# The first product of the gated network with both operand parts in one 512-column matmul, its halves joined by ScalarE and VectorE

## The reference, cut to what matters

```python
h = rmsnorm_2(x, norm2_g[l])
x = x + (jax.nn.silu(h @ ffn_w1[l]) * (h @ ffn_w3[l])) @ ffn_w2[l]
return rmsnorm_2(x, norm_f_g)
```

## Time and profile before

| what | value |
|---|---|
| median of three runs | 1012.93 us (1010.57 to 1013.58) |
| the profiled execution | 1013.9 us, its span 1012.1 us |
| TensorE busy | 977.0 us, 97% of the span, mean granted clock 0.985 |
| VectorE busy | 788.2 us, 78% |
| ScalarE busy | 560.6 us, 55% |
| the `ffn` stage | about 820 to 940 us of the span |

### The profile page before, as it was taken

How to read it: one execution, slowest core, us unless ns; L and a number is a source line. 1 busy time by engine, 2 the same in 40 slices (tenths; PEclk the granted TensorE clock), 3 DMA queues, 4 the chain that set the end, 5 groups by cost and what they waited for, 6 DMA issues and landing times.

```text
span 1012.1 us, 19319 instructions
## 1 busy us (share of the span) xinstructions
PE 977.0 (97%) x7468; PEld 910.6 (90%) x7468; DVE 788.2 (78%) x1370; ACT 560.6 (55%) x922; POOL 105.1 (10%) x134
## 2 busy tenths in 40 slices
PE   4799999999999999999999999999999999999996
PEld 2479998888989899999888999998889999999996
DVE  4757986999777677667876899999998887777554
ACT  3248675444655567776544666677126564444352
POOL 0000000000000000000000000999910000000000
PEclk8799999999999999999999999999999999999998
DMA  9998798887564865554555455453446555555531
GB/s 378 421 419 336 275 378 300 318 325 280 144 203 115 307 239 177 189 186 167 208 179 213 164 193 170 164 208 127 165 139 221 182 187 189 194 179 190 193 116 42
DMA packets 35880, 222.27 MB, mean 220 GB/s; under 512 B 3883, under 2 KB 9180, under 8 KB 9436
## 3 DMA queue, kind: packets, MB, share of 16 engines
q1 hardware_dynamic: 35804, 221.22, 60.6%
HBM read 220.13 MB, written 1.07 MB: 219 GB/s over the span
## 4 chain that ended last, share of the span: by engine, by line
PE 81%; DVE 8%; DMA 4%; ACT 4%; issue 2%; DVEq 0%; SPq 0%; ACTq 0%
PE bank L656 22%; PE bank L645 17%; PE bank L646 16%; PE bank L650 12%; PE bank L982 5%; PE bank L1035 3%; DMA mod_raw<-w_mod 2%; DVE w_lo L1472 2%; PE s_banks L679 1%; ACT w_hi L1109 1%; DVE s_banks L1879 1%; DVE bank L1854 1%; PE s_banks L1035 1%; DMA raw<-weights 1%; DVE ab L1847 1%
## 5 line engine op out<-in xcount | busy, mean ns | idle before, releaser
L1472 DVE TENSOR_TENSOR w_lo<-raw,w_hi 128x1024 fp32r<-128x1024 f32 x284 | 346.3, 1225 | 32.1 <-ACT w_hi L1109 29.7
L1109 ACT ACTIVATE w_hi<-raw 128x1024 fp32r<-128x1024 f32 x284 | 296.1, 1050 | 93.6 <-PE bank L656 89.9
L645 PE MATMUL bank<-xg_hi,w_hi 128*128 128x258 f32 (+1 forms) x1376 | 340.9, 285 | 0.8 <-ACT w_hi L1109 0.5
L646 PE MATMUL bank<-xg_lo,w_hi 128*128 128x258 f32 (+1 forms) x1376 | 336.5, 281 | 0.0
L645 PEld LDWEIGHTS bank<-xg_hi,w_hi 128*128 128x128 f32 x1376 | 259.7, 189 | 5.8 <-issue 4.7
L646 PEld LDWEIGHTS bank<-xg_lo,w_hi 128*128 128x128 f32 x1376 | 260.1, 189 | 0.2
L656 PE MATMUL bank<-xg_hi,w_lo 128*128 128x258 f32 (+1 forms) x1376 | 198.3, 282 | 0.3 <-DVE w_lo L1472 0.3
L656 PEld LDWEIGHTS bank<-xg_hi,w_lo 128*128 128x128 f32 x1376 | 178.5, 189 | 0.8 <-DVE w_lo L1472 0.5
L650 PE MATMUL bank<-hid,w_hi 128*128 128x512 f32 x512 | 127.7, 391 | 0.0
L650 PEld LDWEIGHTS bank<-hid,w_hi 128*128 128x128 f32 x512 | 91.5, 188 | 15.8
L656 PEld LDWEIGHTS bank<-hid,w_lo 128*128 128x128 f32 x512 | 68.5, 188 | 5.3
(11 more groups left out here) (245 smaller groups left out, 1262.0 us busy)
## 6 DMA issues: line engine op xcount, KB each, us to landing
raw<-weights SPq DMA_DIRECT2D x157, 1024.0 KB, 4.9
mod_raw<-w_mod SPq DMA_DIRECT2D x28, 1024.0 KB, 11.4
mod_raw<-w_dots SPq DMA_DIRECT2D x20, 1024.0 KB, 9.6
toep<-bias_by_distance SPq DMA_DIRECT2D x8, 256.0 KB, 5.4
x<-x_in SPq DMA_DIRECT2D x1, 1024.0 KB, 4.9
toep<-bias_by_distance SPq DMA_DIRECT2D x8, 128.0 KB, 3.9
y_out<-yout SPq DMA_DIRECT2D x4, 256.0 KB, 2.4
c_all<-c_row SPq DMA_DIRECT2D x1, 512.0 KB, 14.8
```

The lines of the kernel that those rows point to most:

```text
L645: pe.matmul(dst, hi, r_hi, start=start, stop=False, skip_group_check=True)
L646: pe.matmul(dst, hi, r_lo, start=False, stop=False, skip_group_check=True)
L1109: act.activation(pool_w_hi[:, at, :] if name == "pool" and at < 2 else w_hi[:, at % HL, :], raw[:, slot, (at % 2) * UT * P:(at % 2 + 1) * ...
L1472: ve.tensor_tensor(lo, raw[:, slot, (at % 2) * UT * P:(at % 2 + 1) * UT * P], hi.bitcast(F32), ALU.subtract).then_inc(lo_done, 1)
```

## The change

The high and low part of xg become one tile `xg[P, 2, DC, ROW]`, the high part first. In the `ffn` stage the 16 matmuls over `w_hi` become 8 of 512 columns (`by_high_once`), so that the bank holds two halves. ScalarE copies the second half into `acc2`; VectorE adds the first half to it and then scales the sum by `rstd`. The space behind xg is 64 bytes larger than before, so that `vec` and what follows start 64 bytes later.

```diff
-        half_line("xg_lo")
-        xg_lo = sb("xg_lo", [P, DC, ROW], F32R)
-        with ExitStack() as part:
-            half_line("xg_hi", part)
-            xg_hi = sb("xg_hi", [P, DC, ROW], F32R, part)
-        sb("behind_xg_hi", [P, DC * ROW + 2 * HALF])
+        half_line("xg")
+        xg = sb("xg", [P, 2, DC, ROW], F32R)
+        xg_hi, xg_lo = xg[:, 0], xg[:, 1]
+        sb("behind_xg", [P, 3 * HALF])
...
+        half_copied, halves_added = sem("half_copied"), sem("halves_added")
...
-                            by_high(dst[:, 0:n], slot, k, r_hi[:, k, 0:n], r_lo[:, k, 0:n], k == 0)
+                            if name == "ffn":
+                                by_high_once(dst[:, :], slot, k, xg[:, :, k, 0:n], k == 0)
+                            else:
+                                by_high(dst[:, 0:n], slot, k, r_hi[:, k, 0:n], r_lo[:, k, 0:n], k == 0)
...
-                    by_high(dst[:, 0:n], (U0[name] + j) % HL, k, r_hi[:, k, 0:n], r_lo[:, k, 0:n], k == 0)
+                    if name == "ffn":
+                        by_high_once(dst[:, :], (U0[name] + j) % HL, k, xg[:, :, k, 0:n], k == 0)
+                    else:
+                        by_high(dst[:, 0:n], (U0[name] + j) % HL, k, r_hi[:, k, 0:n], r_lo[:, k, 0:n], k == 0)
...
             def ffn(i, j):
+                act.wait_ge(pe_units, 8 * i + (U0["ffn"] + j + 1))
+                act.wait_ge(tile_read, 8 * i + (T0["ffn"] + j))
+                act.activation(acc2[:], out_bank("ffn", j)[:, SEQ:2 * SEQ], ACT.Copy).then_inc(half_copied, 1)
                 if j % 2 == 0:
...
                 ve.wait_ge(pe_units, 8 * i + (U0["ffn"] + j + 1))
-                ve.tensor_tensor(ab[:, j % 2, 0:SEQ], out_bank("ffn", j)[:, 0:SEQ], rstd[:, 0:SEQ], ALU.mult).then_inc(tile_read, 1)
+                bank, f = out_bank("ffn", j), ab[:, j % 2, 0:SEQ]
+                ve.wait_ge(half_copied, 8 * i + j + 1)
+                ve.tensor_tensor(acc2[:], bank[:, 0:SEQ], acc2[:], ALU.add).then_inc(halves_added, 1)
+                ve.wait_ge(halves_added, 8 * i + j + 1)
+                ve.tensor_tensor(f, acc2[:], rstd[:, 0:SEQ], ALU.mult).then_inc(tile_read, 1)
```

## The result

The changed kernel takes 1023.6 us (median of four runs, 1022.26 to 1025.91) against 1013.15 us beside it: the ratio is 1.0112, 95% interval 1.0096 to 1.0128. It is 1.1% slower, outside the stated range of 1009.5 to 1020. The profiled execution has a span of 1020.8 us, 8.7 more than before.

The account below looks back on a forecast made before the run. TensorE (97% busy) bounds the kernel; in ffn the change makes VectorE the bound. TensorE ends 2.3 us late, moved buffers count 0: 1013.9 becomes 1016.2 profiled, 1015.2 us on the median's scale, range 1009.5 to 1020.

Parts of the forecast that it names:

- The ring: In ffn, copy, addition, silu and splits between ScalarE and VectorE hold a pair of units to at least 5.88 us.
- TensorE's own unit: In ffn, 24 matmuls fall to 2.77 us with 512 columns, saving 2.2 us if TensorE stays the bound.
- Where the lateness goes: From ffn into the last product, banks and splits absorb some lateness; TensorE ends 2.3 us late.
- the split that TensorE needs last: Last ffn unit's split, making low weights for the last product's third unit; done at 949.6, TensorE 2.3 us late.
- The clock: Rival: short TensorE waits in ffn drop the clock to 1.2 GHz, up to 122 us more, 1137; chance 0.02.
- The longer ring: Rival: in ffn the scaling starts 0.56 behind the addition, 0.2 us more a pair, 1019.4 us; chance 0.24.
- TensorE as the bound: Rival: in ffn the odd copy is not held, TensorE sets the pace, 1010.7 us; chance 0.14.
- The places: Rival: moved operands run at 0.91 per eight matmuls in the last product and other stages, about 1009 us; chance 0.10.

Follow-up runs that it names:

- e3: Changed kernel, with ScalarE's silu behind its split instead of ahead of it on even units; 1011.87 us, ratio 0.9992.
- e9: Changed kernel's 512-column matmuls with the eviction of before, reading only the bank's first half (leaves out one product); 1014.4 us, ratio 1.0011.
- e2: Changed kernel, with the last product's first four output tiles in banks 4 to 7, which ffn does not use; 1016.53 us, ratio 1.0029.
- e4: Changed kernel, with 20 idle matmuls into an unused bank ahead of each of the two waits for the last banks; 1022.27 us, ratio 1.0087.
- e6: Changed kernel, with the space behind xg 64 bytes smaller, so everything behind it lies where it lay before; 1024.42 us, ratio 1.0109.
- e10: Changed kernel, with the copied half going to two scratch tiles in turns; 1024.75 us, ratio 1.011.
- e1: Kernel before, with only the buffers placed where the change puts them; 1014.48 us, ratio 1.0014.
- e7: Kernel before, with only the last product's operand (f_hi, f_lo) moved by 128 bytes, to its changed-kernel place; 1011.82 us, ratio 0.9996.
- e5: Changed kernel with the 256-column matmuls of before; ScalarE copies the sum, VectorE takes the greater of sum and copy; 1024.15 us, ratio 1.0105.
- e8: Changed kernel, silu behind the split, everything behind xg in its old place, last product's operand moved 128 bytes; 1011.38 us, ratio 0.999.
- e11: Kernel before, last product's operand moved 128 bytes and TensorE held by a wait in that product's first unit; 1013.78 us, ratio 1.0012.
- e12: Kernel before, with TensorE held by a wait in the last product's first unit, operand in its old place; 1013.49 us, ratio 1.0001.

## Why the prediction was wrong

**The ring: right.** 5.84 us a pair against 5.88, the scaling at 0.46, VectorE's wait of 0.57 against 0.67, ended by ScalarE's copy. The last unit's addition was forecast at 947.6 and stands at 948.55, of which 0.8 is the mixing product's delay ahead of it. TensorE's own unit was forecast at 2.77; free of waits it is 2.787 and `ffn` 1.45 us shorter than before (e3, e9), 0.033 a unit instead of 0.05. TensorE's waits for the low split began some twenty units into the stage (at 871.75), where I had said ten.

**Where the lateness goes: the step that failed.** The prediction said that the split of the last `ffn` unit is "the split that TensorE needs last", and put 2.3 us there. The waits for low splits came, of about that size: 2.7 us against before, all inside `ffn`. But they are not the last wait. The last product's first unit sums four output tiles at once, in the four banks that the last four `ffn` units used, so its third and fourth tile wait for the scaling of the second-last and last unit. TensorE may run four units ahead of the eviction inside `ffn`, and there it loses only 2.7 us against before; at the boundary it must have all four banks within one unit, so everything that it had run ahead is lost at once. That costs 5.4 us, for which the forecast had no term. The kernel before had the same wait, too short to notice: VectorE's last scaling ends at 940.29, and the fourth tile's first matmul runs from 940.37, with 0.20 to the next start instead of 0.12 (the unit took 2.91 for 2.83).

```profile
939.87 0.42 DVE L2050 TENSOR_TENSOR ab<-bank,rstd 128x256 f32<-128x256 f32 x1 [1.26 <-PE bank L656]
```

```profile
940.37 0.36 PE L645 MATMUL bank<-f_hi,w_hi 128*128 128x256 f32 x1
940.57 0.28 PE L646 MATMUL bank<-f_lo,w_hi 128*128 128x256 f32 x1
```

e2 takes this wait out and lands at 1016.5, near the forecast, with 2.76 us more than before in `ffn` and no wait behind it: what I forecast was about a kernel without this bank dependence.

**The clock: a chance of 0.02, and it came, in one place.** I looked at the many short waits inside the stage, where the clock did stay at 1.00. It fell in the one stretch of 5 us with two long waits, for some 7 us, of which TensorE worked the last 4 without a break, and cost 1.7 us (e4). In e6 and e10 it rose later and slowed the second unit as well (3.77 and 3.12 us). The price of 122 us that I gave it was for another event.

**The rivals.** The longer ring would have given 1019.4 by a price (0.56) that the trace refutes (0.46). TensorE as the bound is what e3 shows once the order is changed. The places came within the bounds, both ways: 0.8 and twice 0.5 us lost, 2.2 us won back in the profiled execution, though e1 and e7 show that the place alone does not win them. The mixing product, whose 0.91 for eight was the good case of that rival, itself went to 0.94.

**What it sums to.** On the scale of the profiled executions the forecast was +2.3. Measured are 2.7 in `ffn`, 5.4 the wait at the boundary, 1.7 the clock, 0.8 the mixing product, 1.0 the two `down`, less 2.2 in the last product: 9.6 before rounding. The span shows 8.7, since the other stages took 0.9 less in this execution. The timed runs show more, a ratio of 1.0112 or 11 us. The same sum over the stages is 9.5 us in e5, 10.9 in e6 and 12.1 in e10, the other profiled kernels with this ring: it varies with the rate of the last product (2.1 us) and with how long the clock stays down. So the timed runs lie inside what the profiled ones span. It may be that most of them had the slower rate, but no run shows the rate of an execution that was not profiled.

## What to carry to other kernels

When an edit adds a hand-over between two in-order engines, walk once round the ring with both queues written out, and compare its length with the bound's period; if it is longer, an instruction that waits should not stand ahead of one that others wait for: here moving the silu behind the split was worth the whole loss of 11 us, and a second buffer was worth nothing. If the ring is longer, lateness grows to the depth of the buffering whatever that is, so the question is not only what is late next but where the queue of buffers has to be empty: the place where the next stage takes all the banks at once. Ask of the next stage's first unit which resources it needs, not which of them is the last in the steady state.

## What the runs showed of the hardware

- In the mixing product and the last product the 256-column matmuls (in the rounded format) ran at one of two steady rates, 113.3 or 117.8 ns a matmul (2.72 or 2.83 us for 24), and held it through the stage once the clock was up. In `ffn` before the change it was 117.5 (2.82). In the mixing product the rate goes with the place of the operand in every run (21.8 with the old places, 22.6 with the new). In the last product it needed the new place and a wait of TensorE in the first unit (the changed kernel, e3, e4, e5, e8, e11 against before, e1, e2, e6, e7, e9, e12), and e10 is an exception. What makes it was not found.
- In the second `down` the 256 matmuls of 512 columns took 59.6 us in place of 58.6 by their starts, and the 256 of 256 columns 29.1 in place of 29.5, in every run with the new places; with what lies between the stages, 88.76 against 88.24 us. (The 64 bytes more become a move of 128, since these operands are set by lines of 128 bytes.) The starts of eight and eight now repeat without the two kinds of the earlier trace rows; these are the changed kernel's:

```profile
479.45 2.02 PE L649 MATMUL bank<-hid,w_hi 128*128 128x512 f32 x8
481.31 1.07 PE L655 MATMUL bank<-hid,w_lo 128*128 128x256 f32 x8
482.23 2.02 PE L649 MATMUL bank<-hid,w_hi 128*128 128x512 f32 x8
```

- The granted clock fell to the 1.2 GHz level while TensorE was busy for some 1 of 4 us (944 to 948), and was back at 2.4 GHz before 954. The Trainium skill's page "TensorE: Matmul & The Clock Gate", section "A second HAM failure mode: psum-queue depth-cycling", describes a clock that swings between its levels through short idle spells between groups of matmuls that cycle through banks. This case's trace does not bear that out: from 871 to 942 us TensorE was held up by 0.26 or 0.52 us in every pair of units, over four banks in turns, and the clock stayed at 1.00; it fell only in the stretch with the waits of 2.55 and 1.86 us.
